# A causal depthwise convolution moved from VectorE and GpSimd to TensorE as four-tap diagonal column tiles

## What is computed

```
a, b = jnp.split(u, 2, axis=-1)          # u: 1024 columns of the input projection
g = a * jax.nn.sigmoid(b)
padded = jnp.concatenate([conv_past, g], axis=1)      # 30 rows of past, zeros for the prompt
y = lax.conv_general_dilated(padded, conv_w[:, None, :], window_strides=(1,), padding='VALID',
        dimension_numbers=('NWC', 'WIO', 'NWC'), feature_group_count=512) + conv_b   # width 31
y = jax.nn.silu(layer_norm(y, ln_conv_g, ln_conv_b))  # over the 512 channels
mix = jnp.concatenate([attn, y], axis=-1)             # then mix @ w_out
```

## Time and profile before

| what | us |
|---|---|
| median of 3 runs (lowest, highest) | 1539.68 (1539.55, 1542.5) |
| the profiled execution's own time | 1542.35 |
| its span in the profile | 1540.4 |
| PE busy, share of the span | 1253.4, 81% |
| DVE busy | 754.7, 49% |
| POOL busy | 480.0, 31% |
| ACT busy | 337.0, 22% |
| granted TensorE clock, mean | 0.861 of full |

### The profile page before, as it was taken

One profiled execution on the slowest core, in us unless ns is written; L12 is line 12 of the kernel. 1 busy time (PEld: TensorE's weight loads), 2 busy tenths in 40 slices (PEclk: granted clock), 3 DMA queues, 4 the chain that ended last, 5 costly groups with the idle time before them and its releaser, 6 DMA issues. The chain is left out here.

```text
span 1540.4 us, 13624 instructions
## 1 busy us (share of the span) xinstructions
PE 1253.4 (81%) x4971; PEld 731.2 (47%) x4971; DVE 754.7 (49%) x1541; ACT 337.0 (22%) x756; POOL 480.0 (31%) x292
## 2 busy tenths in 40 slices
PE   4699888947999869999807997895678996999980
PEld 0354425332445457777504544352335453777760
DVE  1109999777525531111152199998774254311114
ACT  2111231142331111111131003312525110211112
POOL 0005999442530020000020079995155011000002
PEclk9799999965699969999958997598557897999995
DMA  9971375330780369999581003011002016599975
GB/s 360 323 245 55 124 279 186 127 155 1 227 286 28 137 221 378 358 365 363 204 300 29 9 27 117 0 63 54 9 1 76 0 55 224 197 362 368 368 261 186
DMA packets 139298, 274.42 MB, mean 178 GB/s; under 512 B 16308, under 2 KB 98588, under 8 KB 132830
## 3 DMA queue, kind: packets, MB, share of 16 engines
q1 hardware_dynamic: 110272, 199.31, 37.6%
q10 hardware_dynamic: 22398, 50.63, 9.7%
q0 software_dynamic: 6560, 23.60, 4.3%
HBM read 237.89 MB, written 52.40 MB: 188 GB/s over the span
## 5 line engine op out<-in xcount | busy, mean ns | idle before, releaser
L409 PE MATMUL ps<-W,arena 128*128 128x256 f32 (+1 forms) x1280 | 346.3, 426 | 8.8 <-DMA W<-in_w_gate 3.4
L409 PEld LDWEIGHTS ps<-W,arena 128*128 128x128 f32 x1280 | 241.2, 192 | 83.8 <-issue 54.3
L419 PE MATMUL ps<-C,arena 128*128 128x128 f32 (+3 forms) x851 | 133.3, 307 | 115.8 <-DVE arena L1310 27.8
L409 PE MATMUL ps<-W,hT 128*128 128x512 f32 (+5 forms) x640 | 192.1, 461 | 1.4 <-DVE gt L1163 1.4
L419 PEld LDWEIGHTS ps<-C,arena 128*128 128x128 f32 (+3 forms) x851 | 111.1, 165 | 155.3 <-issue 58.2
L1237 DVE SCALAR_TENSOR_TENSOR arena<-arena,taps 128x606 f32<-128x606 f32 x180 | 158.9, 952 | 0.2
L1607 POOL TENSOR_TENSOR arena<-arena 128x512 f32<-128x512 f32 x8 | 89.6, 11201 | 211.0 <-ACT arena L897 211.0
L409 PEld LDWEIGHTS ps<-W,hT 128*128 128x128 f32 (+1 forms) x640 | 102.5, 181 | 91.4 <-issue 82.4
L1665 POOL DMA_INDIRECT arena<-y_d,sid x20 | 19.9, 997 | 402.5 <-DMA y_d<-arena 200.8
L647 PE MATMUL ps<-W,hT 128*128 128x512 f32 (+1 forms) x320 | 143.5, 602 | 1.0 <-issue 1.0
L409 PE MATMUL ps<-hT,W 128*128 128x64 f32 (+1 forms) x512 | 141.5, 439 | 3.4 <-ACT hT L868 3.4
(11 more groups left out here) (217 smaller groups left out, 1177.4 us busy)
## 6 DMA issues: line engine op xcount, KB each, us to landing
W<-in_w_ada SPq DMA_DIRECT2D x48, 1024.0 KB, 6.1
W<-in_w_gate SPq DMA_DIRECT2D x32, 1024.0 KB, 10.4
W<-in_w_up SPq DMA_DIRECT2D x32, 1024.0 KB, 13.0
W<-in_w_down SPq DMA_DIRECT2D x32, 1024.0 KB, 7.5
arena<-x_d SPq DMA_DIRECT2D x33, 512.0 KB, 10.9
y_d<-arena ACTq DMA_DIRECT2D x33, 512.0 KB, 7.2
W<-in_w_in SPq DMA_DIRECT2D x16, 1024.0 KB, 14.7
W<-in_w_out SPq DMA_DIRECT2D x8, 1024.0 KB, 6.7
```

The source lines that it names most:

```text
L409: ins = T.matmul(out, l, r, start=n == 0, stop=n == len(pairs) - 1, skip_group_check=True)
L419: count(T.transpose(o, i, ident[0:m, 0:m]), done if n == len(outs_ins) - 1 else None)
```

## The change

The convolution runs on PE. For a block of 128 channels, four groups `g` of 32 channels are four column tiles: the stationary tile `W4` (128 by 32) of a group and of four taps holds the tap values on a diagonal, four times below one another; the moving tile `G4` holds on its partitions 32j to 32j+31 the 32 channels of the group, shifted by j columns. So one matmul with 128 contracted rows adds four taps for 32 channels, and 8 steps `q` do 32 taps (the last is zero). `G4` is filled by 16 DMAs per block from `gT`, issued on SP's queue in between the weight loads (`shifted`). The taps are brought into the form that `W4` needs by 16 small matmuls (into `ps1`, then `tapj`), and POOL builds `W4` by one product of 1024 columns per block. DVE gates straight out of PSUM into `gT`; ACT only takes the sigmoid, and writes the convolution's result with its bias to `cy` (`conv_out`). The LayerNorm of `cy` moves to stages 2 to 4. In layer 0 the bias rows of two `ada` parts (4 DMAs) are issued with the others, ahead of ACT's first work on `hT`.

On SP, between the loads of W (`shifted(0)` ahead of the loads of `c == 3`, 1 and 2 behind them, 3 two loads later in layer 0, behind `c == 4` in layer 1):

```diff
+                def shifted(i):
+
+                    sp.wait_ge(s_glu, 4 * l + i + 1)
+                    if i >= 2:
+                        sp.wait_ge(s_conv, 4 * l + i - 1)
+                    for j in range(4):
+                        for g in range(4):
+                            sp.dma_start(G4[i % 2][32 * j:32 * j + 32, g, 0:634],
+                                         gT[32 * g:32 * g + 32, i, j:j + 634]).then_inc(s_g4[i % 2], 16)
```

On PE:

```diff
+                def conv(i):
+
+                    pe.wait_ge(s_g4[i % 2], (2 * l + i // 2 + 1) * 256)
+                    pe.wait_ge(L["w4"], i + 1)
+                    if i >= 1:
+                        pe.wait_ge(L["cyd"], i)
+                    for b, (s0, n) in enumerate(((0, SEQ), (542, DEC))):
+                        for q in range(NQ):
+                            for g in range(4):
+                                ins = T.matmul(ps[b][32 * g:32 * g + 32, 0:n], W4[:, i % 2, NQ * g + q, :],
+                                               G4[i % 2][:, g, s0 + 4 * q:s0 + 4 * q + n],
+                                               start=q == 0, stop=q == NQ - 1, skip_group_check=True)
+                                count(ins, s_conv if b == 1 and q == NQ - 1 and g == 3 else None)
...
+                    if i == 0:
+                        for g in range(4):
+                            for j in range(4):
+                                ins = T.matmul(ps[1][32 * j:32 * j + 32, 32 * g:32 * g + 32], ident[:, 32 * g:32 * g + 32],
+                                               taps[:, j, :, :].rearrange("p c q -> p (c q)"), start=True, stop=True,
+                                               skip_group_check=True)
...
+                    else:
+                        conv(i - 1)
...
-                    project(c, w, 5 * n, (0, 1, 2), L["proja"], L["proj"])
+                    project(c, w, 5 * n, (3, 4, 7), L["proja"], L["proj"])
+                    if n == 0:
+                        conv(3)
...
+                        pe.wait_ge(L["cyd"], 4)
+                        products(ps[0][:, 0:SEQ], [(ones, cy[:, c, 0:SEQ]) for c in range(4)], L["lnm"])
+                        products(ps[1][:, 0:DEC], [(ones, cy[:, c, SEQ:TOK]) for c in range(4)], L["lnm"])
...
+                    if n == 8:
+                        pe.wait_ge(L["lnsq"], 1)
+                        products(ps[2][:, 0:SEQ], [(ones, sqc[:, c, 0:SEQ]) for c in range(4)], L["lnv"])
+                        products(ps[0][:, 0:DEC], [(ones, sqc[:, c, SEQ:TOK]) for c in range(4)], L["lnv"])
...
-                pe.wait_ge(L["lnr"], 1)
                 turn_qk(qkf, ck, 7)
```

On ACT, DVE and POOL:

```diff
-                    biases(0, 1, 4)
+                    biases(0, 1, 2, 3, 4)
...
+                    if n == 3:
+                        act.wait_ge(L["lnx"], 1)
+                        S.activation(sqc[:, :, :], cy[:, :, :], ACT.Square).then_inc(L["lnsq"], 1)
+                    if n == 15:
+                        act.wait_ge(L["lnr"], 1)
+                        S.activation(lnb[:, :], lnb[:, :], ACT.Sqrt).then_inc(L["lnr"], 1)
...
-                conv(74)
+                for i in range(4):
+                    dve.wait_ge(L["sig"], i + 1)
+                    V.tensor_tensor(gT[:, i, 30:542], ps[3 + 2 * (i % 2)][:, :], sig[:, i % 2, 0:SEQ], ALU.mult)
...
+                    G.tensor_tensor(W4[:, i % 2].rearrange("p (g q) m -> p g q m", g=4),
+                                    C[:, K_M32:K_M32 + 32].unsqueeze(1).unsqueeze(1).to_broadcast(shape),
+                                    tapj[:, :, i, :].unsqueeze(3).to_broadcast(shape), ALU.mult).then_inc(L["w4"], 1)
```

More of the change, by code:

```diff
@@ L120, in program @@
         crows = sb("crows", [62, 512])
-        taps = sb("taps", [P, 4, CW])
+        taps = sb("taps", [P, 4, 4, NQ])
+        tapj = sb("tapj", [P, 4, 4, NQ])
         gq = sb("gq", [P, 2, HD])
@@ L136, in program @@
         route = sb("route", [P, 896])
-        ctmp = sb("ctmp", [P, 2, 606])
-        arena = sb("arena", [P, 22320])
+        stage = sb("stage", [P, 2, 512])
+        arena = sb("arena", [P, 22344])
         def part(at, n, *shape):
@@ L153, in program @@
         kT = [part(8704, 1088), part(9792, 1088)]
[L154 to L158 removed]
+        gT = part(10880, 4 * GW, 4, GW)
+        cy = part(17336, 2304, 4, TOK)
+        msk = part(13440, 1728)
+        XN = part(15168, 5120, NT, D)
+        rel = part(15168, 1728, 3, 576)
+        G4 = [part(3200, 4 * GS, 4, GS), part(6400, 4 * GS, 4, GS)]
+        W4 = part(15168, 2048, 2, 4 * NQ, 32)
         sq = part(0, 3200, NT, 10, HD)
@@ L161, in program @@
         pT = part(19760, 2560, 5, 512)
-        glu = part(19760, 2304, 4, 576)
-        lnb = part(15152, 576)
+        sig = part(20312, 1152, 2, 576)
+        lnb = part(20312, 576)
         sqc = part(10880, 2304, 4, 576)
@@ L169, in program @@
         AB = [part(17336, 2048, 2, D), part(10880, 2048, 2, D)]
-        gf = part(15152, 1024)
+        gf = part(15168, 1024)
         HR = part(5120, 5120, NT, D)
@@ L202, in program @@
         s_pad = sem("s_pad")
+        s_glu, s_conv = sem("s_glu"), sem("s_conv")
+        s_g4 = [sem(f"s_g4{i}") for i in range(2)]
         s_fill = sem("s_fill")
@@ L331, in _, with ada @@
             wexp = [A[n].rearrange("l e (k p) f -> l e p k f", p=P) for n in ("w_gate", "w_up", "w_down")]
-            def ada(first_use, third):
+            def ada(first_use, third, ks=range(KC)):
                 l, q = THIRDS[third]
-                for k in range(KC):
+                for k in ks:
                     load(first_use + k, wada[l, :, k:k + 1, 2048 * q:2048 * q + 2048])
@@ L358, in _ @@
                         load(mixer_use(l, c, hf), src)
+                    if c == 3:
+                        shifted(1)
+                        shifted(2)
+                    if c == 4 and l == 1:
+                        shifted(3)
                 def rows(e):
@@ L1008, in _ @@
                 exps(1)
-                act.wait_ge(L["lny"], 2)
+                act.wait_ge(L["lny"], 1)
                 for c in range(4):
-                    for d, a, n in ((0, 0, SEQ), (SEQ, 542, DEC)):
-                        S.activation(hT[:, 4 + c, d:d + n], cy[:, c, a:a + n], ACT.Silu, bias=vT[:, 48 + c:49 + c],
-                                     scale=vT[:, 44 + c:45 + c]).then_inc(L["mixy"], 1)
+                    S.activation(hT[:, 4 + c, :], cy[:, c, :], ACT.Silu, bias=vT[:, 48 + c:49 + c],
+                                 scale=vT[:, 44 + c:45 + c]).then_inc(L["mixy"], 1)
                 for n, (t, g) in enumerate(GROUPS):
@@ L1151, in _ @@
             V.memset(scT[:, :, :], 0.0).then_inc(s_pad, 1)
+            V.memset(taps[:, :, :, :], 0.0)
+            V.memset(stage[:, :, :], 0.0).then_inc(s_pad, 1)
             V.memset(small[:, :], 1.0).then_inc(s_init, 1)
```

177 lines of the change are left out of this document (71 added, 106 removed).

## The result

| | median us | lowest to highest | runs |
|---|---|---|---|
| before | 1539.62 | 1535.74 to 1542.5 | 4 |
| changed | 1576.7 | 1575.21 to 1578.11 | 4 |

The ratio is 1.0241, with a 95% interval of 1.0222 to 1.0259: slower. 1568 was forecast, with 1546 to 1594 as the range. The profiled execution of the changed kernel took 1576.5 us (1542.35 before), its span is 1574.3 us (1540.4 before).

A forecast was written before the change was run, and what follows sets the result against it. PE was taken as the bound everywhere but the score stage and tail, where DVE was. Layer 0's +15.9 and layer 1's +13.0 made +28.9 on 1542.35: 1571.3, or 1568 on the medians' footing, range 1546 to 1594.

The forecast's parts named there:

- A block on TensorE: Convolution on PE: 6.9 us of 512-column steps plus 1.5 of 64-column steps, 8.4 a block (7.8 to 13.5), all on the path.
- The shifted copies: SP's 16 DMAs a block: 2 us of waiting once, for layer 0's first block (0 to 10); later blocks covered.
- The bias DMAs: Four more issues by ACT before its first work on hT, layer 0 only: 2.21 us, all on the path.
- The score stage: Without taps and POOL beside it: 42 us against 56.4 in layer 0, 36 in layer 1; 14.4 and 14.0 saved.
- the stall behind score 20: Score stage: DVE's 6.4 us of reciprocal and product at n = 20 outlast the six scores PE may run ahead.
- The index transposes: LayerNorm's first sums (4.54 us) go where PE waits 5.61 us for the rope: no cost.
- The tail: Ahead of the q and k transposes: DVE's variance wait goes, POOL's rope ends it; 8.2 us saved in layer 0, 7.6 layer 1.
- Dearer steps: Rival, convolution: 64-column steps at upper bound, 41 us more, 1609; different-weight quarters not side by side, 1733; chance 0.11.
- Nothing back in the score stage: Rival: the LayerNorm's chain stalls the three-deep ring of scores and the stage keeps its length: 1596 us; chance 0.09.
- The clock on the other side: Rival: shorter tail leaves PE's clock up, attention shrinks, some 20 us a layer: 1528 us, faster; chance 0.10.
- PE's gap ahead of the first block: Sign, convolution: no PE row waits for the DMAs of G4, except perhaps the first.
- the stretch between layer 0's transposes and layer 1: Outside the forecast's stages; a change of over 5 us in such a stage's length would show the forecast wrong.

## Why the prediction was right, point by point

The mechanism was as forecast and the likeliest case came. The sum was 28.9 us against 34.2 on the profiled executions (37.1 by the medians). That it came so near is in part luck. The copies were 13.9 us dearer than their term and the score stages gave 4.5 less; the blocks were 4.0 cheaper, the index transposes gave 6.2 that no term had, and 3.7 came off in stretches that the sum left out.

- **A block on TensorE, 8.4 us:** 7.9. The large part was right. The 64-column steps go at the lower bound, 0.11 us each, so 1.5 was 0.9 or so. 31.6 us a layer, not 33.6. Doubling the steps cost their full length (+63.5), so "it stands on the path" was right too. The column tiles with four different weights paid no weight load: by the rule of the Trainium skill, "TensorE: Matmul & The Clock Gate", section "Part 3: Packing small matmuls — row/col tiling", that the prediction cites, a block would have taken 7.9 + 2.1 = 10 us, an estimate, and the measurement decides against it here. (The same section also lets a load into the background weight buffer run ahead; no row here tells whether that is what happened.)
- **The shifted copies, 2 us once:** 15.9 us, the term that was mis-sized most, and beyond its stated bound of 10. The issues took 0.7 us each, not 0.4, and without the fill 0.66, with no wait; the landing took 20.4 us beside the fill, where the forecast took 10 from two loads of another kind. It was in the right place and for the right cause (the fill), as the run without it shows, and it also drew half-clock time behind it, which was not counted.
- **The bias DMAs, 2.2:** their issues took 2.13, and the start of the products moved by 2.3, which lies near the scatter of 1.8 among kernels with the same code there.
- **The score stage, -14.4 and -14.0:** -12.0 and -11.9. The term reckoned with the stall behind score 20, but gave it too little; without reciprocal and product in the ring the stages are 4.8 us shorter each.
- **The index transposes, nothing:** -3.0 and -3.2. From the state transposes to the first score it took 12.3 us before (175.40 to 187.69) and 9.3 after. Two things did it, about half each. DVE's rope, first and last row of it before and after, ends 6.1 us behind its start before and 3.9 after; the kernel with POOL's taps left out has 3.9 too, so it is POOL that was in its way:

```profile
175.93 2.28 DVE L297 TENSOR_TENSOR arena<-arena,C 128x320 f32<-128x320 f32 x4 [2.12 <-ACT iw L882]
181.78 0.23 DVE L301 TENSOR_TENSOR arena<-arena 64x80 f32<-64x80 f32 x1
```

```profile
226.68 1.70 DVE L302 TENSOR_TENSOR arena<-arena,C 128x320 f32<-128x320 f32 x4 [58.25 <-ACT iw L933]
230.30 0.23 DVE L306 TENSOR_TENSOR arena<-arena 64x80 f32<-64x80 f32 x1
```

  And the sums of the LayerNorm keep PE at work in what was its wait, and its transposes then took 2.81 us at a granted clock of 1.00, not 4.37 (0.72). PE's transposes start 0.8 us behind the end of the rope, held up by the sums, so "nothing" was nearly right for the sums themselves; what the forecast lacked is the clock and the rope.
- **The tail, -8.2 and -7.6:** -8.0 and -7.5, with POOL's L306 as the new end of the wait, as forecast. The condition that the forecast named, that reciprocal and product no longer follow, was needed as well: with the wait alone removed nothing is won.
- **The rivals.** Dearer steps: refuted by 7.9 us. Nothing back in the score stage: refuted by 24 us back. The clock on the other side: refuted. In the attention of layer 1 it stayed at its lower level; first row layer 0, second layer 1, of the changed kernel:

```profile
357.49:397.49 40.00, 28.79 (x93) 14.32 (x93) 25.65 (x94) 18.97 (x43) 11.25 (x12) 0.54 0.10 34
1117.45:1196.15 78.70, 59.07 (x207) 30.82 (x208) 56.15 (x188) 33.73 (x83) 25.18 (x21) 0.52 0.15 40
```

  78.7 us, as in the earlier trace rows. The idle time ahead of it is longer than before, 25.33 us against 12.78, as the forecast's argument against this rival had it.

By layers: +27.8 at layer 0's transposes and +9.85 in layer 1, where +15.9 and +13.0 were forecast. Of the forecast's own signs, PE's gap ahead of the first block, longer than its bound, did show, and the stretch between layer 0's transposes and layer 1, which the sum left out, changed by 5.05 us, just over the size that it named as a sign of being wrong. Why it did stays open. The kernels tried here that have one expert tile in layer 0's overflow loop take 485.7 to 496.8 us for it, some with little changed there, so 5 us lie within what this stretch varies by; no run was aimed at it.

## What to carry to other kernels

Work taken off an engine that nobody waits for buys nothing: DVE's 71 taps under a busy PE were free, and TensorE paid 7.9 us for each block it took over; what helped was POOL's leaving, a shorter DVE queue and an earlier LayerNorm, and all of that could be had with one block on TensorE (1512) rather than four (1577). When a wait goes, look at what the engine that ended it has queued behind it: here the wait's removal was worth nothing until that went too. For a DMA that others wait for, read the landing of the same kind of transfer in an empty and in a full queue before pricing it, and keep bulk transfers that nobody awaits out of that stretch.

## What the runs showed of the hardware

- **DVE kept POOL out for as long as it ran without a break.** In the kernel before, POOL's fourth gate product fell beside DVE's taps; POOL in order of time:

```profile
116.62 1.26 POOL L1607 TENSOR_TENSOR arena<-arena 128x512 f32<-128x512 f32 x1 [15.76 <-ACT arena L897]
133.93 41.01 POOL L1607 TENSOR_TENSOR arena<-arena 128x512 f32<-128x512 f32 x1 [15.77 <-ACT arena L897]
```

  1.26 us alone, 41.01 beside them. DVE's taps end at 173.80 and it then waits 2.12 us for ACT; POOL's product ends at 174.94, 1.14 us into that pause, so it can have done nearly all of its work there. DVE's taps kept 0.76 us meanwhile. In the score stage, where both have short pauses, DVE pays as well: its taps take 1402 ns and not 841. The rows look like a lock and not like sharing. The Trainium skill, "SBUF — State Buffer", section "SBUF: two separate sides", has it as an exclusive lock on a port pair between GpSimd and a DVE operation with two SBUF inputs, held for the whole instruction. The rows agree, and show in addition that POOL seems to have got no turn between some 52 (39.87 us / 0.76) back-to-back DVE instructions.
- **Column tiles with different weights, f32.** Four side by side, 128 by 32 weights each; the groups of one block of layer 1 in the changed kernel (count, busy us, mean ns, idle us ahead):

```profile
L519 PE MATMUL ps<-arena 128*32 128x512 f32 x64 | 7.1, 594 | 0.0
...
L519 PE MATMUL ps<-arena 128*32 128x64 f32 x64 | 1.1, 218 | 0.0
```
